# Nine landing buffers for gathered expert rows, and the lower parts of expert tiles shared between GpSimd and VectorE

## The chip, the core and the metric

The kernel runs on one core of one Trainium2 chip. The metric is the device time of one execution in microseconds (us), from the first instruction to the last; lower is better. The engines are TensorE (PE, with its weight loads as PEld), VectorE (DVE), ScalarE (ACT), GpSimd (POOL) and SyncE (SP). SP, ACT and POOL also issue DMAs.

## The reference, cut to what matters

One layer for 512 prompt tokens and 32 sample tokens (width 1024): two kinds of attention, then PEER, a layer of 128 x 128 = 16384 experts that are one neuron each. Only PEER matters here:

```python
def peer(x):                       # 544 tokens
    q = x @ w_query                # 8 heads; two halves scored against 128 sub keys each
    v1, i1 = top_k(s1, 16); v2, i2 = top_k(s2, 16)
    cand = v1[..., :, None] + v2[..., None, :]
    top, pos = top_k(cand, 16)     # 16 experts per head: 128 per token
    eidx = i1 * 128 + i2           # taken at pos
    g = softmax(top)
    hid = einsum("thkd,td->thk", u_tab[eidx], x)
    a = g * gelu(hid)
    return einsum("thk,thkd->td", a, v_tab[eidx])
```

## The kernel before, in words

**Two ways through the experts.** The last 384 prompt tokens take the dense way: TensorE multiplies them with all 128 tiles of the up table (a tile is 128 experts x 1024), ScalarE applies gelu, and the result goes to DRAM (`hidden_values`). A gate matrix, made from one-hots of the expert numbers, goes to DRAM too (`gate_matrix`), and a later stage multiplies both and the value table `v`. The first 128 prompt tokens and the 32 sample tokens take the sparse way: their expert rows are gathered one by one. A "row" of that work is 5 gathers (`ROW`): 4 for prompt tokens, 1 for the sample tokens spread over 128 partitions; each gather brings 128 table rows of 4 KB into one buffer of `gb`. There are 32 such rows (`SR`), 160 gathers, and for each a **dot** on VectorE (`dot`, L1837 to L1843): buffer times the tokens' activations in PSUM (`x2p`), summed.

**float32 products in three passes.** TensorE multiplies rounded parts. A tile `uw` is split into `uhi` (ScalarE rounds it, `u_split_hi`, L1317) and `ulo = uw - uhi` (`u_split_lo` on GpSimd, L1322, or `split_lo` on VectorE, L1851), and `mm3` (L224 to L228) adds hi*hi, lo*hi and hi*lo. `uhi` and `ulo` have two buffers each, `uw` has four (`UR`). So tile m+2 can be rounded only when product m is done, and its `ulo` has to be there when product m+1 is.

**The query stage** (the block from L1410) runs eight turns with 4 tiles each, then a tail of 16 tiles (`QX`). GpSimd makes every `ulo` here. VectorE picks the experts. In the tail ScalarE turns the gate logits into exponentials after tile 11 (`MIX = 11`, L1518 to L1520), which needs another activation table than gelu; VectorE normalizes them; SP spreads the sample tokens' indices and gates over the partitions; VectorE writes the first five rows of indices (`idx_row`, L1670), and GpSimd issues the first five gathers between its last splits. A block ends when all engines have ended.

**The gate stage** (the block from L1737) has 72 tiles in six turns of 12 (`GTI`), two turns to a pass of a hardware loop for the first four and the last two written out, and then 8 more tiles (`GX`), here called the tail. Per turn of 12 tiles:

- TensorE does the 12 products in halves and, between them, 16 groups of four one-hot products (L1778).
- VectorE does for each tile: the split `ulo` of tile i+2; the one-hots of one or two groups (`build_one_hots`: `oh` L1830, `og` L1831; every second group has its `oh` from ScalarE); two dots (three in the last tile), 25 in a turn.
- ScalarE does gelu and its store (L1340, L1342), `uhi` (L1320), the eviction of each group (L1936), half of the `oh` (L1910, L1914), and twice a turn the store of 2 MB of gates (L1927).
- GpSimd issues a gather as soon as the dot that frees its buffer is done (`fetch_u_row`, L1363): five gathers are under way or waiting for VectorE. It cuts the one-hots' numbers twice a turn (`cut`, L1791).
- SP loads the tiles `uw`. At the stage's start it also loads four value tiles into `vw`.

The tail's 8 products come with no groups. VectorE does the last ten dots there, three to a tile, then the lower parts of the four value tiles, then the last split. Its last lines wait for the first products with the gates. ScalarE ends the block with a wait for all gelu stores (L1963, L1964). The value stage (from L1998) then takes its first tiles at once.

## Time and profile before

| | us |
|---|---|
| three runs | 1894.58, 1899.97, 1898.62 (median 1898.62) |
| the profiled execution, its own time | 1890.6 |
| its span, first to last instruction | 1889.0 |
| TensorE busy in the span | 1715.0 (91%) |
| VectorE busy | 1400.6 (74%) |
| ScalarE busy | 783.8 (41%) |
| GpSimd busy | 594.3 (31%) |

The mean TensorE clock granted is 0.956 of full speed. The parts of the span that are spoken of below: the end of the query stage, from about 805 to 838 us; the gate stage's 72 tiles from 838.4 to 1287.1 us; its tail to 1328.3 us; a wait between blocks to 1338.6 us; then the value stage to the end, 550 us.

A group of instructions is named by line, engine, operation, the tile that it writes and the tiles that it reads. In a timeline, the first column is the start in us, the second what it took, and in brackets stands how long the engine had been idle before it and what ended that.

### The profile page before, as it was taken

To read this page: it belongs to the slowest core of one execution; us is meant where nothing else is said; L and a number is where in the kernel's file an instruction comes from. 1 tells how busy PE (TensorE), PEld (TensorE's weight loads), DVE (VectorE), ACT (ScalarE), POOL (GpSimd) and SP (SyncE) were. 2 spreads that over 40 slices of the span, in tenths; PEclk is the share of its full clock that TensorE was granted. 3 is DMA by queue.
4 is the path that set the end of the run, shared out by engine and by line. 5 is a ranking of instruction groups with operands and counts; after the bars stand their busy time and mean duration, and the time that the engine had idled before them with its cause. 6 is when DMAs were issued, how large, how long until landed. Compare 5 with 4: busy or idle time off the path is not lost. (4 is left out here: it accounts for less than half of the span.)

```text
span 1889.0 us, 30318 instructions
## 1 busy us (share of the span) xinstructions
PE 1715.0 (91%) x9914; PEld 1501.5 (79%) x9914; DVE 1400.6 (74%) x3171; ACT 783.8 (41%) x1195; POOL 594.3 (31%) x516
## 2 busy tenths in 40 slices
PE   5997898789799999979889899998799999999995
PEld 4997643449699999969889898997688888888883
DVE  3334267534399999939898898997799999999994
ACT  3231044211434342337566576664233333333333
POOL 0010270000344534633333334333333333333330
PEclk9998899889799999989999999998899999999997
DMA  3352461260343432458999999999999999999991
GB/s 110 98 181 80 138 192 46 107 242 5 119 148 103 147 99 96 158 204 320 345 330 338 342 360 343 373 367 332 341 382 384 384 384 384 384 386 386 387 383 62
DMA packets 195215, 470.82 MB, mean 249 GB/s; under 512 B 17922, under 2 KB 100482, under 8 KB 192558
## 3 DMA queue, kind: packets, MB, share of 16 engines
q1 hardware_dynamic: 124014, 240.30, 36.5%
q0 software_dynamic: 50944, 178.96, 25.6%
q10 hardware_dynamic: 20160, 50.34, 6.7%
q8 instruction: 52, 0.85, 0.2%
q14 instruction: 45, 0.37, 0.1%
HBM read 411.97 MB, written 61.32 MB: 251 GB/s over the span
## 5 line engine op out<-in xcount | busy, mean ns | idle before, releaser
L226 PE MATMUL hp<-mid_hi,uhi 128*128 128x384 f32 x1024 | 361.4, 353 | 23.6 <-DVE ulo L1853 8.5
L227 PE MATMUL hp<-mid_lo,uhi 128*128 128x384 f32 x1024 | 351.1, 343 | 0.0
L228 PE MATMUL hp<-mid_hi,ulo 128*128 128x384 f32 x1024 | 349.7, 342 | 0.0
L226 PE MATMUL va<-vhi,ahi 128*128 128x512 f32 x768 | 299.8, 390 | 10.4 <-PEq L1734 10.4
L228 PE MATMUL va<-vhi,alo 128*128 128x512 f32 x768 | 299.5, 390 | 0.0
L227 PE MATMUL va<-vlo,ahi 128*128 128x512 f32 x768 | 299.5, 390 | 0.0
L1712 POOL DMA_INDIRECT gathered<-in_v_experts,idx_row x160 | 189.2, 1183 | 329.2 <-DVEq L2060 284.9
L1369 POOL DMA_INDIRECT gathered<-in_u_rows,idx_row x160 | 171.8, 1074 | 299.5 <-DVE hrow L1840 208.1
L1720 ACT ACTIVATE vhi<-vw 128x1024 fp32r<-128x1024 f32 x128 | 135.9, 1062 | 256.8 <-PE va L228 145.3
L226 PEld LDWEIGHTS hp<-mid_hi,uhi 128*128 128x128 f32 x1024 | 198.4, 194 | 28.7 <-issue 15.5
L1320 ACT ACTIVATE uhi<-uw 128x1024 fp32r<-128x1024 f32 x128 | 135.6, 1059 | 167.1 <-PE hp L228 114.6
L227 PEld LDWEIGHTS hp<-mid_lo,uhi 128*128 128x128 f32 x1024 | 198.3, 194 | 0.0
L228 PEld LDWEIGHTS hp<-mid_hi,ulo 128*128 128x128 f32 x1024 | 197.7, 193 | 0.0
L1840 DVE CUSTOM_DVE_ANT_0 gathered<-gathered,x2p 128x1024 f32<-128x1024 f32 x150 | 177.9, 1215 | 22.9 <-DMA gathered<-in_u_rows,idx_row 20.2
L226 PEld LDWEIGHTS va<-vhi,ahi 128*128 128x128 f32 x768 | 144.7, 188 | 40.7 <-issue 10.7
L1324 POOL TENSOR_TENSOR ulo<-uw,uhi 128x1024 fp32r<-128x1024 f32 x50 | 125.0, 2501 | 148.8 <-ACT uhi L1320 148.8
L227 PEld LDWEIGHTS va<-vlo,ahi 128*128 128x128 f32 x768 | 144.7, 188 | 30.1
L228 PEld LDWEIGHTS va<-vhi,alo 128*128 128x128 f32 x768 | 144.6, 188 | 30.1
L1724 DVE TENSOR_TENSOR vlo<-vw,vhi 128x1024 fp32r<-128x1024 f32 x128 | 156.1, 1221 | 12.9 <-ACT vhi L1720 11.8
L2057 DVE SCALAR_TENSOR_TENSOR acc<-gathered,crow,acc 128x1024 f32<-128x1024 f32 x128 | 164.1, 1282 | 0.7 <-DVE acc L2057 0.7
L1778 PE MATMUL ggp<-og,oh 128*128 128x128 f32 x768 | 106.8, 283 | 30.4 <-DVE og L1831 29.6
L1778 PEld LDWEIGHTS ggp<-og,oh 128*128 128x128 f32 x768 | 97.8, 193 | 43.0 <-DVE og L1831 25.7
(331 smaller groups left out, 3281.8 us busy)
## 6 DMA issues: line engine op xcount, KB each, us to landing
uw<-in_u_experts SPq DMA_DIRECT2D x128, 512.0 KB
vw<-in_v_experts SPq DMA_DIRECT2D x128, 512.0 KB
hidden_values<-gelu_out ACTq DMA_DIRECT2D x128, 192.0 KB
gate_matrix<-gst ACTq DMA_DIRECT2D x12, 2048.0 KB
hd<-hidden_values SPq DMA_DIRECT2D x16, 768.0 KB
gt<-gate_matrix SPq DMA_DIRECT2D x16, 768.0 KB
uw<-hidden_values SPq DMA_DIRECT2D x16, 768.0 KB
uw<-gate_matrix SPq DMA_DIRECT2D x16, 768.0 KB
```

The lines of the kernel that those rows point to most:

```text
L226: nc.tensor.matmul(out, a_hi, b_hi, start=first, stop=False)
L227: nc.tensor.matmul(out, a_hi, b_lo, start=False, stop=False)
L228: return nc.tensor.matmul(out, a_lo, b_hi, start=False, stop=last)
L1320: nc.scalar.activation(uhi[:, i], uw[:, r], ACT.Copy).then_inc(u_hi, 1)
L1324: nc.gpsimd.tensor_tensor(ulo[:, i], uw[:, r], uhi[:, i].bitcast(F32), ALU.subtract).then_inc(u_lo, 1)
L1369: nc.gpsimd.indirect_dma_start(gb[:, b], None, u_table, bass.IndirectOffsetOnAxis(ap=idx_row[:, slot, b:b + 1], axis=0)).then_inc(gathered ...
L1712: nc.gpsimd.indirect_dma_start(gb[:, b], None, v_table, bass.IndirectOffsetOnAxis(ap=idx_row[:, slot, b:b + 1], axis=0)).then_inc(gathered ...
L1720: nc.scalar.activation(vhi[:, c], vw[:, c], ACT.Copy).then_inc(xs["vhi"], 1)
L1724: nc.vector.tensor_tensor(vlo[:, c], vw[:, c], vhi[:, c].bitcast(F32), ALU.subtract).then_inc(xs["vlo"], 1)
L1778: last = nc.tensor.matmul(gp[i % 2][:, k], oh[:, i % RING, k], og[:, i % RING, k], start=True, stop=True)
L1840: nc.vector.tensor_tensor_reduce(out=gb[:, b], in0=gb[:, b], in1=x2p[:, b // SG], scale=1.0, scalar=0.0, op0=ALU.mult, op1=ALU.add, accum_ ...
L2057: nc.vector.scalar_tensor_tensor(acc0[:], gb[:, c], crow[:, q, c:c + 1], acc0[:], ALU.mult, ALU.add).then_inc(s["s0"], 1)
```

## The change

Five things change together.

1. **Nine buffers.** The four `vw` buffers, idle in the gate stage, join the five of `gb` (`buffers`, `LOOK = 9`). Nine rows of indices are prepared, nine gathers are issued at the end of the query stage, and a gather waits for the dot nine before it. Five dots now stand ahead of the turns (`FIRST_DOTS`), a turn has 25 and 20 dots in alternation (25 in each of the last two), and 15 instead of 10 stand in the tail. These 15 gathers use only the five `gb` buffers. The four value tiles are loaded when dot 145 is done, not at the stage's start.
2. **The splits.** In the 72 tiles GpSimd makes `ulo` at every odd i, VectorE at every even i. At the query stage's end VectorE makes two that were GpSimd's, and the last one moves behind the barrier, to the head of the gate stage.
3. **The exponential** comes after tile 13 (`MIX = QX - 3`), and two more `uw` loads stand before the spreading of the indices on SP.
4. **The wait for all gelu stores** goes from ScalarE at the end of the block to SP at the start of the value stage.
5. The value stage's gathers have semaphores of their own (no effect on the work).

The core of the diff:

```diff
-        MIX = 11
+        MIX = QX - 3
+        buffers = [gb[:, b] for b in range(ROW)] + [vw[:, i] for i in range(GT)]
+        FIRST_DOTS = ROW
+        TURN_ROWS = (ROW, ROW - 1)
...
-                for e in range(QX):
+                for e in range(QX - 3):
                     u_split_lo(pool, RT * NH + e + 2, e % 2, (e + 2) % UR)
-                    if e == QX - 3:
-                        for b in range(3):
-                            fetch_u_row(pool, 0, 0, b)
-                    if e == QX - 2:
-                        for b in range(3, ROW):
-                            fetch_u_row(pool, 0, 0, b)
+                for n in range(LOOK):
+                    request(pool, n)
...
 # GpSimd, a turn of the gate stage
-                        while at < RJ * ROW * (i + 1) // GTI:
-                            q, b = divmod(at, ROW)
-                            fetch_u_row(pool, RJ * j + q + 1, (q + 1) % RJ, b)
+                        if i % 2:
+                            m = G0 + GTI * j + i + 2
+                            pool.wait_ge(u_lo, m + 2)
+                            u_split_lo(pool, m, i % 2, slot(half, i + 2))
+                        while at < n * (i + 1) // GTI:
+                            ahead = half * ROW * ROW + at + LOOK
+                            if not last or ahead < 2 * ROW * ROW:
+                                request(pool, FIRST_DOTS + ahead, pair)
...
 # VectorE, a turn of the gate stage
-                        split_lo(G0 + GTI * j + i + 2, i % 2, slot(half, i + 2))
+                        if i % 2 == 0:
+                            dve.wait_ge(u_lo, G0 + GTI * j + i + 4)
+                            split_lo(G0 + GTI * j + i + 2, i % 2, slot(half, i + 2))
...
 # VectorE, head of the gate stage
+                dve.wait_ge(s["x2p"], 2)
+                split_lo(G0 + 1, 1, 1)
+                for n in range(FIRST_DOTS):
+                    dot(n, hid[:, n // ROW, n % ROW:n % ROW + 1])
                 for i in range(AHEAD):
                     build_one_hots(0, i)
...
 # ScalarE, end of the gate stage
-                for i in range(2):
-                    act.wait_ge(ge_stored[i], 8 * NK + 16)
...
 # SP, gate stage
-                for i in range(GT):
-                    sp.dma_start(vw[:, i], A["v_experts"][i]).then_inc(vld[i], 16)
...
+                    if e == UR + 1:
+                        sp.wait_ge(s["dot"], TAIL)
+                        for i in range(GT):
+                            sp.dma_start(vw[:, i], A["v_experts"][i]).then_inc(vld[i], 16)
```

**GpSimd's order in a turn.** The first tiles of a turn in the loop. Before, it has the cut and gathers alone (rows that only compute a wait's value are the `ISA` and `REGISTER_ALU` ones):

```order
L1796 COPY chunkT<-slotT 128x96
L1367 REGISTER_ALU
L1369 DMA gathered<-in_u_rows,idx_row 128x1024
L1367 REGISTER_ALU
L1369 DMA gathered<-in_u_rows,idx_row 128x1024
L1367 REGISTER_ALU
L1369 DMA gathered<-in_u_rows,idx_row 128x1024
```

and now:

```order
L1829 COPY chunkT<-slotT 128x96
L1842 ISA
L1324 REGISTER_ALU
L1325 TENSOR_TENSOR ulo<-uw,uhi 128x1024
L1377 REGISTER_ALU
L1383 DMA vw<-in_u_rows,idx_row 128x1024
L1377 REGISTER_ALU
L1383 DMA vw<-in_u_rows,idx_row 128x1024
L1377 REGISTER_ALU
L1383 DMA gathered<-in_u_rows,idx_row 128x1024
L1377 REGISTER_ALU
L1383 DMA gathered<-in_u_rows,idx_row 128x1024
```

A split now stands behind the gathers of the tile before it and ahead of those of its own tile: four gathers (of an odd and an even tile), then the next split.

**VectorE's order at the head of the gate stage.** Before, right behind the barrier:

```order
L1830 TENSOR_SCALAR oh<-iota,chunkT 128x128
L1831 TENSOR_SCALAR og<-iota,chunkT 128x128
L1830 TENSOR_SCALAR oh<-iota,chunkT 128x128
L1831 TENSOR_SCALAR og<-iota,chunkT 128x128
L1830 TENSOR_SCALAR oh<-iota,chunkT 128x128
```

and now:

```order
L1897 TENSOR_TENSOR ulo<-uw,uhi 128x1024
L1397 ISA gathered,hid<-gathered,x2p 128x1024
L1397 ISA hid 128x1
L1397 ISA gathered,hid<-gathered,x2p 128x1024
L1397 ISA hid 128x1
```

The first one-hots move behind one split and five dots (an `ISA` row that reads `gathered` and `x2p`, and the short one that reads its sum, are one dot).

## Rows read from the trace of the kernel before

**Rows 1.** Stretches: us, busy (count) of PE, PEld, DVE, ACT, POOL; PEclk; DMA share; GB/s.

```profile
838.40:1287.10 448.70, 413.37 (x2522) 399.82 (x2523) 396.31 (x979) 292.43 (x480) 162.51 (x158) 0.97 0.93 344
1287.10:1338.60 51.50, 32.65 (x168) 31.08 (x167) 29.47 (x46) 16.20 (x24) 15.93 (x14) 0.84 0.94 358
...
1600.00:1700.00 100.00, 100.00 (x442) 82.78 (x442) 92.06 (x111) 37.35 (x49) 35.41 (x31) 1.00 1.05 384
```

**Rows 2.** Waits in 840:1290: who waited for whom, us, times, longest.

```profile
DVE gathered L1840 <- DMA gathered<-in_u_rows,idx_row: 20.2, 12, 3.7
ACT gelu_out L1340 <- DMA hidden_values<-gelu_out: 17.3, 5, 4.4
```

**Rows 3.** Timeline, one event in the gate stage, and TensorE at the loop's jump back.

```profile
927.09 1.22 DVE L1840 CUSTOM_DVE_ANT_0 gathered<-gathered,x2p 128x1024 f32<-128x1024 f32 x1 [3.53 <-DMA gathered<-in_u_rows,idx_row]
928.54 0.49 ACT L1340 ACTIVATE gelu_out<-hp 128x384 f32<-128x384 f32 x1 [3.48 <-DMA hidden_values<-gelu_out]
930.77 2.05 PE L1778 MATMUL ggp<-og,oh 128*128 128x128 f32 x8 [4.77 <-DVE og L1831]
991.42 0.68 PE L226 MATMUL hp<-mid_hi,uhi 128*128 128x384 f32 x1 [4.94 <-issue]
```

**Rows 4.** ScalarE's timeline: gelu after three tiles in a row, one `uhi`, the next gelu.

```profile
1102.17 0.49 ACT L1340 ACTIVATE gelu_out<-hp 128x384 f32<-128x384 f32 x1 [0.95 <-PE hp L228]
1107.80 0.49 ACT L1340 ACTIVATE gelu_out<-hp 128x384 f32<-128x384 f32 x1 [0.78 <-PE hp L228]
1108.96 1.06 ACT L1320 ACTIVATE uhi<-uw 128x1024 fp32r<-128x1024 f32 x1 [0.66 <-ACT gelu_out L1340]
1119.19 0.49 ACT L1340 ACTIVATE gelu_out<-hp 128x384 f32<-128x384 f32 x1 [1.02 <-PE hp L228]
```

**Rows 5.** Timeline, VectorE from one split to the next, and GpSimd's two gathers.

```profile
1104.70 1.22 DVE L1853 TENSOR_TENSOR ulo<-uw,uhi 128x1024 fp32r<-128x1024 f32 x1
1110.95 1.22 DVE L1853 TENSOR_TENSOR ulo<-uw,uhi 128x1024 fp32r<-128x1024 f32 x1
1104.37 0.94 POOL L1369 DMA_INDIRECT gathered<-in_u_rows,idx_row  x1 [2.44 <-DVE hrow L1840]
1105.62 1.11 POOL L1369 DMA_INDIRECT gathered<-in_u_rows,idx_row  x1 [0.30 <-issue]
```

**Rows 6.** One line each: instances, ns min/median/max, first and last start.

```profile
L1324 POOL TENSOR_TENSOR ulo<-uw,uhi x50: 2347/2406/3516, 494.1 to 832.6; 128x1024 fp32r<-128x1024 f32 x50
L1641 DVE TENSOR_TENSOR pk<-eq x8: 324/326/2303, 549.1 to 805.3; 128x160 f32<-128x160 bf16 x8
```

**Rows 7.** Timeline, GpSimd and VectorE: splits, and VectorE's two operations of the same size.

```profile
808.61 0.83 DVE L1651 TENSOR_TENSOR GG<-GG,first 128x640 f32<-128x640 f32 x1
811.23 2.36 POOL L1324 TENSOR_TENSOR ulo<-uw,uhi 128x1024 fp32r<-128x1024 f32 x1 [3.83 <-ACT uhi L1320]
811.53 2.75 DVE L1663 TENSOR_TENSOR GG<-GG,sm 128x640 f32<-128x640 f32 x1
```

**Rows 8.** Timeline, end of the query stage: ScalarE, GpSimd, TensorE.

```profile
809.47 0.74 ACT L1520 ACTIVATE GG<-GG 128x640 f32<-128x640 f32 x1 [2.59 <-DVE GG L1651]
832.63 2.35 POOL L1324 TENSOR_TENSOR ulo<-uw,uhi 128x1024 fp32r<-128x1024 f32 x1
838.42 0.68 PE L226 MATMUL hp<-mid_hi,uhi 128*128 128x384 f32 x1 [8.34 <-PEq L1372]
```

**Rows 9.** Timeline, the tail: VectorE, TensorE, ScalarE's last gelu and next work.

```profile
1289.98 1.22 DVE L1853 TENSOR_TENSOR ulo<-uw,uhi 128x1024 fp32r<-128x1024 f32 x1
1295.87 1.22 DVE L1880 CUSTOM_DVE_ANT_0 gathered<-gathered,x2p 128x1024 f32<-128x1024 f32 x1 [4.66 <-DMA gathered<-in_u_rows,idx_row]
1303.34 0.69 PE L226 MATMUL hp<-mid_hi,uhi 128*128 128x384 f32 x1 [7.65 <-DVE ulo L1853]
1328.29 0.49 ACT L1340 ACTIVATE gelu_out<-hp 128x384 f32<-128x384 f32 x1 [1.68 <-PE hp L228]
1338.47 1.03 ACT L2027 ACTIVATE acc<-h 128x1024 f32<-128x1024 f32 x1 [9.69 <-PEq L1734]
```

More of the change, by code:

```diff
@@ L1696, in build @@
         vld = [sem(f"x_vld{i}") for i in range(GT)]
+        row_landed = [sem(f"x_row{b}") for b in range(ROW)]
         gld = [sem(f"x_gld{i}") for i in range(2)]
@@ L1770, in _, with turn @@
                 pe.sem_inc(s["mm"], RING)
-                def turn(j, half, last):
+                def turn(pair, half, last):
+                    j = 2 * pair + half
                     def group(i):
@@ L1796, in cut, with turn @@
                     nc.gpsimd.tensor_copy(chunkT[:, u], slotT[:, :, bass.ds((2 * j + u) * CH, CH)]).then_inc(s["cut"], 1)
-                def turn(j, half, last):
+                def turn(pair, half, last):
+                    j = 2 * pair + half
+                    n = (ROW if last else TURN_ROWS[half]) * ROW
                     at = 0
@@ L1916, in _, with turn @@
                 first_one_hot(0, 1)
-                def turn(j, half, last):
+                def turn(pair, half, last):
+                    j = 2 * pair + half
                     def tile(i, part):
@@ L1939, in group @@
                             first_one_hot(j, i + 2)
-                        elif i % 2 and not last:
+                        elif i % 2 and not (last and half):
                             first_one_hot(j + 1, i + 2 - N2)
@@ L1962, in _, with turn @@
                             round_a(act, c, c, 0)
[L1963 to L1964 removed]
             @block.sync
             def _(sp):
[L1968 to L1970 removed]
+                def turn(pair, half, last):
+                    j = 2 * pair + half
                     for i in range(GTI):
```

134 lines of the change are left out of this document (83 added, 51 removed).

## The prediction, made before the run

> **What bounds the kernel now.** I first cut the span into stretches. The gate stage's 72 tiles take 448.7 us, with TensorE busy for 413 and VectorE for 396, the DMA engines at a share of 0.93; the 51.5 us behind them hold only 32.7 us of TensorE [rows 1]. So neither engine alone fills the stage. Next I took the pitch of undisturbed tiles from ScalarE's timeline, where each gelu starts when its product is done: three tiles, from 1102.17 to 1119.19, take 17.02 us [rows 4]. 24 such groups would be 408.5 us, so about 40 us are lost. Of these I see three kinds in the timelines. The first product runs at TensorE's lower clock (3 us), and at the loop's jump back TensorE stands for 4.94 us with nothing to wait for and starts at half speed (0.68 us for a matmul), together about 6 [rows 3]; neither is touched. Of the other 31 us, small gaps take some 3, and 28 stand around ten places where VectorE waits for a gather. In all it waits 20.2 us in 12 places, and ScalarE 17.3 us in 5 places for its own gelu stores [rows 2]. The largest shows how this counts: VectorE waits 3.53 us, the one-hots come late, TensorE stands for 4.77 us and starts again at half speed (2.05 us for a group that takes 1.13 otherwise, the 1.2 GHz level) [rows 3].
>
> **The change, part by part.** The sum is made against the profiled execution, 1890.6 us (span 1889.0). That is 8.0 us under the median of the three runs; I add these at the end.
>
> *End of the query stage: -1 us.* ScalarE no longer waits 2.59 us for the logits after tile 11 [rows 8], and two `uw` loads come earlier. But the block ends with its last engine. Before, that was GpSimd with a split (832.63 + 2.35); 3.4 us later TensorE starts, at 838.42 [rows 8]. Now GpSimd has nine gathers to issue, 1.25 us each [rows 5], 11.5 us in all, and it can start only when the indices are there. The exponential (now near 815), sum, reciprocal, product, the new split of 1.2 us and the spreading of the gates bring these to about 822. 822 + 11.5 = 833.5, against 835.0. The ends are -4 and +3.
>
> *Head of the gate stage: +3 us.* VectorE waits for `uhi` (1.1), then does one split and five dots (1.14 each) and only then the first one-hots. The first group is ready about 10 us after the start. TensorE's first product, at the low clock, is done after 7.3 us. Ends: +1 and +6.
>
> *Nine buffers: -20 us.* A buffer is asked for again nine dots ahead, not five; a dot comes every 2.7 to 3 us, so a gather has some 25 us, not 14, to land, and the waits of up to 3.7 us [rows 2] go. What is late next is ScalarE's own wait: two gelu buffers, and a gelu store that queues behind 2 MB of gates. In rows 3 it stands beside the gather's wait (3.48 us). It delays `uhi` and the evictions, and I leave 8 us of the 28 for it: five places, 1.6 each. The traffic does not fall: 25 gathers of 0.52 MB, twelve tiles and the stores are 26 MB a turn, at the value stage's 384 GB/s [rows 1] 67 us, just a turn of 68. Ends: -30 (all goes, and with it the cold clock), -10 (ScalarE's waits grow, as the gather queue is never empty).
>
> *Lighter VectorE: -3 us.* In clean groups TensorE still waits 0.26 us for `og`, once in three tiles; with six splits fewer a turn this and a little more goes. Ends -6 and 0.
>
> *Splits on GpSimd: +17 us.* This is the term I weigh most. The split itself takes 2.41 us there [rows 6] instead of 1.2. I laid out six tiles. A product's end is P; gelu starts at P + 0.1, `uhi` starts 1.16 later (1107.80 to 1108.96) and is done at P + 2.3 [rows 4], 0.7 later where ScalarE evicts. The split must be done when the next product ends, P + 6.0 to 6.4. Alone, GpSimd would be in time: 2.3 + 2.5 = 4.8. But the gathers of the even tile before stand ahead of it, and they wait for VectorE's dots. VectorE begins an even tile with its split at P + 2.2 and, where the tile has two groups, ends its dots 6.25 later (1104.70 to 1110.95 [rows 5]), at P + 8.45. GpSimd has the second gather issued some 2.1 after the last dot (the dot ends just before the split at 1104.70, the gather at 1105.62 + 1.11 = 1106.73 [rows 5]), at P + 10.55. Its split ends at P + 13.1. The next product's end, 5.4 later, plus 6.0 gives a due time of P + 11.4. TensorE waits 1.7 us. In the two other pairs of the six tiles the same sum comes out at or just under the due time. So 1.7 us per six tiles, 12 times: 20 us. Some of it falls together with ScalarE's waits; I take 17. Ends: 3 (requests in time, as VectorE runs ahead) and 38 (the lock below in each pair).
>
> The port: VectorE's `pk` takes 326 ns, and 2303 once [rows 6]; in that one a GpSimd split was under way. Of two equal operations on `GG`, one took 0.83 us and the other, begun 0.3 us after a GpSimd split, 2.75: it ended 0.7 after the split had [rows 7]. So a VectorE operation with two inputs in SBUF stands still behind a GpSimd split. In the gate stage the dots have one input in PSUM, and the two engines' splits exclude each other in time anyway. For the one-hots the trace shows no such pair; the sum assumes a loss inside the slack that VectorE gains. The Trainium skill (SBUF - State Buffer, "Who interferes with whom") says more: a `tensor_scalar` in a 2-port mode contends with GpSimd as well, and whoever comes first blocks the other fully. By that rule every GpSimd split that meets one-hots holds VectorE up to 2.4 us; this is the second rival below.
>
> *The tail: +3 us.* Before, from the last of the 72 products to the value stage's start it took 51.5 us [rows 1]: 41.2 to the last product, then ScalarE's wait for all gelu stores, which held the block from 1328.8 to about 1335 (its next work is at 1338.47 [rows 9]). That wait now delays no engine but SP: -7. Against this, the queue of gathers runs dry: the first of the last 15 waits for dot 145, some 6 us behind product 72. 15 gathers are 7.9 MB; four value tiles, now in the same stretch, are 2.1; `uw` loads, first gates and gelu stores some 4. 14 MB at 0.384 MB/us [rows 1] is 36 us, so the last gather lands near 42 us. Then come a dot, four lower parts of value tiles (4.6), the last split, a product (4.2), the barrier (3.4): 57 us, so +6. The other end is -7, if gathers come as asked. I take +3, nearer to the ledger; upper end +10. The waits before the last products (4.66 us, with TensorE idle for 7.65 [rows 9]) turn into more and shorter ones.
>
> *The value stage* has the same work. SP's wait for gelu stores ends before the tiles of the third group are due: 0.
>
> Sum: -1 + 3 - 20 - 3 + 17 + 3 = -1. 1890.6 - 1 + 8.0 = **1897.6 us**, no change that can be measured. A measurement of this kernel can tell about 0.3% (5.7 us) from nothing.
>
> **The rivals.** *Waits gone, GpSimd in time.* If VectorE's dots run ahead (B turns have only 20), or the gathers are issued faster, the 17 shrinks to about 3 and the 20 grows to 26: with the tail at 0 this is -27 us, 1871. For it: 36 splits of 1.2 us leave VectorE's 396 us [rows 1]; gathers are the largest wait. Against it: VectorE's even tile always begins with a split that waits for `uhi`, so it can't run ahead there.
>
> *GpSimd's queue and the lock (slower).* The place is the odd tile, the price is what the split waits for. If one-hots are held too, VectorE loses 2.4 us in two of three pairs: 4.8 - 3.5 (the splits given away) = 1.3 us more work per six tiles than before, each late one-hot stops TensorE, and the clock falls behind long waits. With 38 for 17 and the gathers' gain at 15, the sum is +26: 1924. It decides as soon as the wait before every second `ulo` is over 2.5 us per six tiles. For it: rows 6 and 7. Against it: by my layout most GpSimd splits lie beside dots.
>
> *The gathers were not the cause.* If the losses come from ScalarE's store waits, nine buffers bring only -5; with a share of the rest this is +12, 1910. For it: five of the large losses have both waits. Against it: five small ones have only the gather's.
>
> **How the numbers follow.** The balance as summed: 0.37 (inside it a third each falls to faster, same, slower, the same a little more). Waits gone: 0.32. Queue and lock: 0.19. Store waits: 0.12, all slower. Faster by over 0.3%: 0.32 + 0.11 = 0.43. Within: 0.17, with 0.02 from the rivals' edges 0.19. Slower: 0.38. The range reaches from the faster rival with the tail's other end (-7 us: 1864) to the slower rival (1924); beyond either I leave one in ten.
>
> **What would show it.** Right: VectorE's waits for gathers in the 72 tiles fall from 20 us to under 4; GpSimd's `ulo` starts 1 to 3 us after its `uhi` in the odd tile behind two groups, and TensorE's idle time names GpSimd's `ulo` with 10 to 25 us; the first one-hots come 8 us after the barrier; from product 72 to the value stage 50 to 58 us. Wrong: three tiles in 16.8 us throughout, no wait on GpSimd's `ulo` (faster); or one-hots of over 1 us beside GpSimd splits and a stage over 460 us (slower).

## The result: slower, and where the time went

The changed kernel takes 1912.97 us, the median of five runs (1910.02 to 1915.19), against 1898.62 for the kernel before in the same series. The ratio is 1.0084, with a 95% interval from 1.0071 to 1.0098: 14.4 us, or 0.84%, slower. That lies inside the recorded range, but it is neither the forecast (no change) nor the side to which most of the chance was given.

The profiled run of the changed kernel is 1912.35 us (span 1910.8). The profiled run of before was 8.0 us under its median, so the two spans differ by 21.8 us where the medians differ by 14.4. The ledger below explains the 21.8, and up to 7 us of it are scatter.

The stretches of the changed kernel, which answer to [rows 1]: from TensorE's first product of the gate stage to the gelu that the prediction took as the end of 72 tiles (by count of gelus it is the one behind product 73, in both kernels), and from there to the value stage. The columns are start and end, length, busy time and count of PE, PEld, DVE, ACT and POOL, granted clock, DMA share, GB/s.

```profile
843.00:1296.95 453.95, 409.78 (x2522) 398.51 (x2523) 417.91 (x935) 294.30 (x482) 225.34 (x183) 0.98 0.91 326
1296.95:1360.00 63.05, 33.38 (x168) 31.78 (x166) 34.73 (x54) 16.42 (x24) 23.40 (x21) 0.82 0.96 354
```

I go on calling them the 72 tiles and the tail. The 72 tiles grew by 5.3 us and the tail by 11.5. VectorE lost 36 splits of 1.2 us and is still busy for 21.6 us more.

The waits in the same part of the program (840 to 1300 us): who waited for whom, us in all, times, longest.

```profile
PE hp L226 <- POOL ulo L1325: 24.5, 19, 4.8
PE ggp L1811 <- DVE og L1873: 19.6, 15, 3.9
...
ACT gelu_out L1341 <- DMA hidden_values<-gelu_out: 4.5, 2, 3.0
```

VectorE's wait for gathers, 20.2 us in [rows 2], is gone from this list. In its place TensorE waits 24.5 us for lower parts that GpSimd makes.

The timeline of one such wait, in the changed kernel: start, length, engine, line, operation.

```profile
911.93 0.94 POOL L1383 DMA_INDIRECT gathered<-in_u_rows,idx_row  x1 [0.30 <-issue]
...
912.37 2.99 DVE L1872 TENSOR_SCALAR oh<-iota,chunkT 128x128 f32<-128x128 f32 x1
...
912.89 2.38 POOL L1325 TENSOR_TENSOR ulo<-uw,uhi 128x1024 fp32r<-128x1024 f32 x1
...
915.29 0.34 DVE L1873 TENSOR_SCALAR og<-iota,chunkT 128x128 f32<-128x128 f32 x1
915.33 0.44 PE L226 MATMUL hp<-mid_hi,uhi 128*128 128x384 f32 x1 [1.24 <-POOL ulo L1325]
```

Two things stand here together. GpSimd's split comes right behind a gather, and TensorE waits for it. And a one-hot of VectorE, 0.28 us elsewhere, lasts 2.99 us, until the split is done.

The end of the query stage and the tail, in the changed kernel's timeline, which answer to [rows 8, 9].

```profile
817.67 0.82 DVE L1690 TENSOR_REDUCE sm<-GG 128x40 f32<-128x640 f32 x1 [3.94 <-ACT GG L1545]
825.16 1.12 POOL L1383 DMA_INDIRECT gathered<-in_u_rows,idx_row  x1 [11.78 <-DVE idx_row L1702]
835.39 0.94 POOL L1383 DMA_INDIRECT vw<-in_u_rows,idx_row  x1 [0.30 <-issue]
842.66 0.26 POOL L1829 COPY chunkT<-slotT 128x96 f32<-128x96 f32 x1 [6.33 <-DVEq L1861]
843.00 0.68 PE L226 MATMUL hp<-mid_hi,uhi 128*128 128x384 f32 x1 [15.41 <-PEq L1400]
...
1298.31 0.95 POOL L1383 DMA_INDIRECT gathered<-in_u_rows,idx_row  x1 [2.11 <-DVE hrow L1397]
1308.57 1.22 DVE L1397 CUSTOM_DVE_ANT_0 gathered<-gathered,x2p 128x1024 f32<-128x1024 f32 x1 [8.21 <-DMA gathered<-in_u_rows,idx_row]
1316.60 0.69 PE L226 MATMUL hp<-mid_hi,uhi 128*128 128x384 f32 x1 [11.37 <-DVE ulo L1897]
```

The nine gathers start at 825.16, not at the 822 of the prediction, and end at 836.3. TensorE, whose last product was done at 827.3, stands for 15.4 us. The first one-hots follow a split and five dots, as forecast, and TensorE waits for them:

```profile
852.80 1.90 PE L1811 MATMUL ggp<-og,oh 128*128 128x128 f32 x8 [3.91 <-DVE og L1873]
```

In the tail the first of the last fifteen gathers is asked for at 1298.31, VectorE waits 8.21 us for its row, and TensorE 11.37 us for a split behind it. VectorE's last dot begins at 1337.34 and the last product ends at 1350.8. Then TensorE stands still once more, before its first product of the value stage:

```profile
1360.04 0.76 PE L226 MATMUL va<-vhi,ahi 128*128 128x512 f32 x1 [9.24 <-PEq L1767]
```

### The profile page after: what moved, and what is told of

It reads as the page before. It is cut to its first block and busy times, and to the rows that moved or that the text cites. A ratio compares the mean times of both kernels' runs of the same rounds, so it can differ in the third digit from the quotient of the medians.

```text
span 1910.8 us, 30365 instructions
## 1 busy us (share of the span) xinstructions
PE 1711.9 (90%) x9914; PEld 1500.2 (79%) x9914; DVE 1430.8 (75%) x3137; ACT 785.4 (41%) x1195; POOL 661.3 (35%) x549
## 5 line engine op out<-in xcount | busy, mean ns | idle before, releaser
L1325 POOL TENSOR_TENSOR ulo<-uw,uhi 128x1024 fp32r<-128x1024 f32 x83 | 204.5, 2464 | 155.7 <-ACT uhi L1321 155.0
L1383 POOL DMA_INDIRECT gathered<-in_u_rows,idx_row x96 | 98.1, 1022 | 150.2 <-DVE hrow L1397 93.9
L1990 ACT ACTIVATE gst<-ggp 128x512 f32<-128x512 f32 x96 | 108.5, 1130 | 61.9 <-PE ggp L1811 48.5
L1397 DVE CUSTOM_DVE_ANT_0 gathered<-gathered,x2p 128x1024 f32<-128x1024 f32 x96 | 114.6, 1216 | 17.1 <-DMA gathered<-in_u_rows,idx_row 15.4
L1873 DVE TENSOR_SCALAR og<-iota,chunkT 128x128 f32<-128x128 f32 x384 | 123.2, 365 | 0.0
```

Of the source, the lines that this page charges most:

```text
L1325: nc.gpsimd.tensor_tensor(ulo[:, i], uw[:, r], uhi[:, i].bitcast(F32), ALU.subtract).then_inc(u_lo, 1)
L1397: nc.vector.tensor_tensor_reduce(out=buffers[to], in0=buffers[to], in1=x2p[:, b // SG], scale=1.0, scalar=0.0, op0=ALU.mult, op1=ALU.add, ...
L1873: last = nc.vector.tensor_scalar(og[:, i % RING, k], iota[:], col(0), col(2), ALU.is_equal, ALU.mult)
L1990: nc.scalar.activation(gst[:, u, :, 4 * r:4 * r + 4].rearrange("p i t -> p t i"), gp[i % 2][:], ACT.Copy).then_inc(s["ev"], 1)
```

## The experiments

Each kernel was timed beside the kernel before in at least five rounds. Ratios are to the kernel before, with their 95% intervals; a gain from one experiment to the next is the difference of their ratios. The theories at the start: GpSimd's splits cost time, either because VectorE's operations stand still beside them, as at an SBUF port that both engines use (**P**, port), or by their place in GpSimd's queue (**Q**; experiments 1 and 2 do not part the two yet); and **B**, the gather waits were slack and the buffers bring nothing. Tail, head and barrier have theories of their own.

**1. All splits of the turns back on VectorE.** The changed kernel with this edit:

```diff
 # GpSimd's turn
-                        if i % 2:
...
-                            u_split_lo(pool, m, i % 2, slot(half, i + 2))
 # VectorE's turn
-                        if i % 2 == 0:
-                            dve.wait_ge(u_lo, G0 + GTI * j + i + 4)
-                            split_lo(G0 + GTI * j + i + 2, i % 2, slot(half, i + 2))
+                        split_lo(G0 + GTI * j + i + 2, i % 2, slot(half, i + 2))
```

> The changed kernel with one part undone: VectorE makes the lower parts of all 72 tiles in the turns again, and GpSimd none; nine buffers, the later exponential and the tail stay as changed. Theory P (port): GpSimd's splits cost the stage what the nine buffers give, since VectorE's one-hots stand still beside them (0.28 us became 3.00 us) and since a split stands behind gathers. VectorE then gets 36 splits of some 1.14 us back (41 us) and loses some 57 us of slowed one-hots; the 72 tiles take 435 to 445 us (453.9 in the changed kernel, 448.7 before), and the run 1898 to 1906 us. The rival B (buffers): the gather waits were slack of VectorE and the nine buffers bring nothing; the 72 tiles take 448 to 454 us and the run 1908 to 1914 us. In both the way from the last product of the turns to the value stage stays some 60 us.

Measured: 1.0041 (1.0028 to 1.0054), 1899.5 us. Its stretches, and the one kind of wait for a DMA in its 72 tiles:

```profile
843.99:1284.64 440.65, 414.35 (x2522) 400.40 (x2523) 391.05 (x969) 292.60 (x481) 146.57 (x147) 0.97 0.91 336
1284.64:1347.10 62.46, 35.15 (x169) 33.86 (x167) 35.52 (x56) 16.34 (x24) 23.11 (x21) 0.80 0.96 359
```

```profile
ACT gelu_out L1341 <- DMA hidden_values<-gelu_out: 19.2, 6, 4.7
```

The 72 tiles take 440.7 us: 13.3 under the changed kernel and 8.0 under the kernel before. Theory B falls. GpSimd's splits cost 13 us of this stretch, and 8 us by the ratios; the rest of the loss is in the tail (62.5 us) and at the end of the query stage.

**2. The splits on GpSimd alone,** on the kernel before, five buffers kept; the same lines as in experiment 1, put in.

> The kernel before with one part of the change alone: GpSimd makes the lower parts of every second tile in the turns, five buffers and all else as before. Theory P: slower than before by 10 to 25 us (1908 to 1924), some one-hots of VectorE last 1 to 3 us beside a split of GpSimd, and VectorE's busy time in the 72 tiles does not fall although it makes 36 splits fewer. Rival B: the splits on GpSimd are neutral, and the run stays at 1897 to 1901 us; the loss of the whole change then lies in its head and tail.

Measured: 1.0060 (1.0040 to 1.0081). The 72 tiles take 460.7 us, 12 more, although this profiled run was one of the kernel's fastest (1898.9). VectorE is busy for 425.7 us of them (396.3 before) with 36 splits fewer; TensorE waits 32.9 us for GpSimd's lower parts. So the splits cost about the same with five buffers (11 to 12 us) as with nine.

**3. The wait for the last gelu stores alone,** on the kernel before.

```diff
 # ScalarE, end of the gate block
-                for i in range(2):
-                    act.wait_ge(ge_stored[i], 8 * NK + 16)
 # SyncE, start of the value block
+                for i in range(2):
+                    sp.wait_ge(ge_stored[i], 8 * NK + 16)
```

> The kernel before with one part of the change alone: the wait for the two last gelu stores moves from the end of ScalarE's gate block to SyncE's start of the value block. By the prediction's term it gives 7 us back (1891 to 1893 us). The rival, by the changed kernel's trace, in which 9.2 us still lie between the last product and the first of the next block: the blocks' change itself takes that long, and the run stays at 1897 to 1900 us.

Measured: 0.9996 (0.9981 to 1.0011). Nothing comes back: TensorE still stands for 10.83 us ahead of the first value product (10.39 in the kernel before). A gain of 7 us would be a ratio of 0.9963 and lies outside the interval.

```profile
1341.15 0.77 PE L226 MATMUL va<-vhi,ahi 128*128 128x512 f32 x1 [10.83 <-PEq L1734]
```

**4. The order of the last buffers,** on the kernel of experiment 1.

```diff
-            users = [n for n in range(TAIL) if n % LOOK == t % ROW] + [TAIL + q for q in range(t % ROW, t, ROW)]
+            to = (t + 1) % ROW
+            users = [n for n in range(TAIL) if n % LOOK == to] + [TAIL + q for q in range(t % ROW, t, ROW)]
```

The gather goes to buffer `to`, and VectorE's dots of the tail take the same one (not shown).

> The first of these kernels (all splits of the turns on VectorE) with the last fifteen gathers sent to the buffers in the order 1, 2, 3, 4, 0 and not 0 to 4: the first of them then waits for dot 137 and not for dot 145, the fifth for 145. Theory T (dry queue): the tail is long because the first of the last gathers is behind the last dot of the turns; here four of them are under way by then, VectorE's wait of 8.2 us for the first row falls to under 2 us, the way from the last product of the turns to the value stage falls from some 60 to 50 to 55 us, and the run is 5 to 10 us below the first kernel. The rival: rows land no faster than one in 1.25 to 2.6 us beside the loads of the value experts, the first wait goes and later ones grow, and the run is within 2 us of the first kernel.

Measured: 0.9997 (0.9985 to 1.0009), 1891.6 us, 0.0044 or some 8 us below experiment 1. The profile shows both theories at work: the first wait is gone, and one of 4.52 us appears later. The stretch ends at 57.6 us, not at the 51.5 of [rows 1].

```profile
1281.05:1338.60 57.55, 34.98 (x168) 33.38 (x167) 35.52 (x56) 16.43 (x24) 19.34 (x17) 0.86 0.96 362
```

```profile
1294.65 1.22 DVE L1398 CUSTOM_DVE_ANT_0 gathered<-gathered,x2p 128x1024 f32<-128x1024 f32 x1 [4.52 <-DMA gathered<-in_u_rows,idx_row]
1296.69 0.94 POOL L1383 DMA_INDIRECT gathered<-in_u_rows,idx_row  x1 [4.81 <-DVE hid L1398]
...
1299.81 0.69 PE L226 MATMUL hp<-mid_hi,uhi 128*128 128x384 f32 x1 [6.29 <-DVE ulo L1894]
```

**5. The first one-hots ahead of the first five dots,** on experiment 4.

```diff
                 split_lo(G0 + 1, 1, 1)
+                for i in range(AHEAD):
+                    build_one_hots(0, i)
                 for n in range(FIRST_DOTS):
                     dot(n, hid[:, n // ROW, n % ROW:n % ROW + 1])
-                for i in range(AHEAD):
-                    build_one_hots(0, i)
```

> The same kernel (all splits on VectorE, new order of the last buffers, 1891.6 us) with VectorE's first two sets of one-hots ahead of its first five dots. In the one without, TensorE stood 3.9 us for the first set at 853.8 us and ran the group at half clock behind it (1.99 us and not 1.2). Theory H (head): that wait goes and the run is 3 to 5 us shorter (1887 to 1889). The rival: the wait only moves, since the five dots then stand ahead of the next split (5.7 us), and the run stays within 1 us.

Measured: 0.9962 (0.9946 to 0.9977); the 72 tiles fall from 439.5 to 433.3 us. The order at the head costs 6 us.

```profile
842.59:1275.89 433.30, 410.11 (x2522) 396.54 (x2523) 390.86 (x969) 292.14 (x481) 150.69 (x151) 0.98 0.94 346
```

**6. No gather ahead of the barrier,** on experiment 5: the loop over `request` moves from the query block to behind the first chunk copy of the gate block.

> The kernel with one-hots first, in which also all nine first gathers are asked for behind the barrier and the first chunk copy, not ahead of the barrier. Theory N (nine gathers): before the barrier GpSimd issues nine gathers in some 11.3 us from 825 us on, and the last product of the query stage ends at 828; without them TensorE starts the gate stage 7 to 10 us earlier (15.6 us of idle time become 6 to 8), the first rows land some 8 us later than now against the dots, and the run is 4 to 8 us shorter (1881 to 1885). The rival: the dots, 9 us later, hold up VectorE's splits in the first tiles, and the run is within 2 us of the kernel without.

Measured: 0.9929 (0.9910 to 0.9948), 0.0033 or 6 us below experiment 5. TensorE's idle time between the blocks falls from 15.9 to 1.9 us, and the stage starts 12.7 us earlier in the profile (829.86); but its 72 tiles take 442.8 us, not 433.3. Both theories are half right: the start is won, and 9.5 of the 12.7 us are given back in the profiles, about half by the ratios.

```profile
829.86:1272.65 442.79, 414.86 (x2522) 401.10 (x2523) 391.64 (x969) 292.05 (x481) 161.04 (x160) 0.97 0.94 349
```

**7. Gelu stores on SyncE's queue,** on experiment 6.

```diff
 # ScalarE's turn
-                            hidden_gelu(act, m, i % 2)
+                            hidden_gelu(act, m, i % 2, store=False)
 # SyncE's turn
+                        store_gelu(sp, G0 + GTI * j + i - 2, i % 2)
                         u_fetch(sp, G0 + GTI * j + i + UR, slot(half, i))
```

`store_gelu` waits for the gelu and stores its result; the first and last tiles, which are changed to match, are not shown.

The reason was the chain of one wait in experiment 1, in time order over four engines: a store of gates, the gelu that waits for an earlier gelu's store, VectorE behind it, TensorE behind that.

```profile
1140.47 0.34 ACTq L1975 DMA_DIRECT2D gate_matrix<-gst  x1
1155.65 0.49 ACT L1341 ACTIVATE gelu_out<-hp 128x384 f32<-128x384 f32 x1 [3.54 <-DMA hidden_values<-gelu_out]
1157.98 1.23 DVE L1893 TENSOR_TENSOR ulo<-uw,uhi 128x1024 fp32r<-128x1024 f32 x1 [2.70 <-ACT uhi L1321]
1161.08 2.07 PE L1811 MATMUL ggp<-og,oh 128*128 128x128 f32 x8 [2.68 <-DVE og L1869]
```

> The kernel with late requests, in which SyncE's queue stores the gelu results of the 72 tiles, not ScalarE's, on which they stand behind the 2 MB stores of the gate matrix. With all splits on VectorE there is one wait of ScalarE for a gelu store of 3.5 to 4.7 us per turn of twelve tiles, 15 us behind the issue of a gate store, and behind it TensorE stands 2.7 to 3.1 us for one-hots and runs eight matmuls at half clock (2.07 us and not 1.16). Theory S (stores): these waits go, and the run is 10 to 16 us shorter than without. The rival: the stores wait behind the 0.5 MB loads of expert tiles on SyncE's queue, or the DMA engines (0.92 busy) are what is short; the run is within 4 us.

Measured: 0.9779 (0.9757 to 0.9800), 1852.2 us: 28 us below experiment 6 and 42 below the kernel before. This is the version that beats both kernels.

```profile
833.82:1246.32 412.50, 399.98 (x2522) 394.12 (x2523) 390.30 (x969) 285.24 (x482) 156.39 (x160) 0.99 0.99 376
```

The 72 tiles take 412.5 us, 30.3 less than in experiment 6. TensorE's wait for `og`, 18.0 us there, is 2.9. The DMA share is 0.99; that the traffic is the next bound was not tried.

The gain is far above the 10 to 16 us expected, and the edit did more than its theory says. ScalarE's waits for gelu stores fall from 21.1 to 10.5 us only. But ScalarE had also stood some 0.6 us behind every gelu, to see it finished and to issue the store, before it could round the next tile. In experiment 6:

```profile
ACT uhi L1321 <- ACT gelu_out L1341: 41.1, 71, 0.7
```

In experiment 7 this wait is gone from the 72 tiles, and three tiles in a row with no disturbance take 16.35 us, where they took 17.06 (ScalarE's rows of the same tiles, experiment 6 and then 7):

```profile
941.53 0.49 ACT L1341 ACTIVATE gelu_out<-hp 128x384 f32<-128x384 f32 x1 [0.96 <-PE hp L228]
958.59 0.49 ACT L1341 ACTIVATE gelu_out<-hp 128x384 f32<-128x384 f32 x1 [1.03 <-PE hp L228]
...
939.90 0.49 ACT L1345 ACTIVATE gelu_out<-hp 128x384 f32<-128x384 f32 x1 [0.98 <-PE hp L228]
956.25 0.49 ACT L1345 ACTIVATE gelu_out<-hp 128x384 f32<-128x384 f32 x1 [1.05 <-PE hp L228]
```

Undisturbed threes are 0.5 to 0.7 us shorter throughout the stage, so by my estimate 12 to 17 of the 30 us come from the shorter cycle and the rest from the store waits. No run parts the two.

**8. Work on GpSimd that nobody waits for,** on experiment 4.

```diff
 # GpSimd's turn
+                        if i % 2:
+                            pool.wait_ge(spare_done, GTI // 2 * j + i // 2 + 1)
+                            nc.gpsimd.tensor_tensor(spare[:], spare[:], spare[:], ALU.subtract).then_inc(spare_done, 1)
```

> The kernel with all splits on VectorE and the new order of the last buffers (1891.6 us), in whose turns GpSimd also does, in every second tile where the changed kernel has its split, a subtraction of the same size over a buffer of its own that nobody waits for. It parts two ways in which GpSimd's splits cost: theory P (port): VectorE's one-hots stand still while GpSimd subtracts, whoever uses the result; then some one-hots last 1 to 3 us, VectorE's busy time in the 72 tiles rises by 40 us or more from 391 us, and the stage by 6 to 14 us (run 1897 to 1906). Theory Q (queue): the cost is TensorE's wait for a split that stands behind two gathers; nothing waits here, so the stage grows by 0 to 3 us (run 1890 to 1895), and one-hots beside GpSimd's work stay near 0.3 us.

Measured: 1.0306 (1.0282 to 1.0329), 59 us more than experiment 4, far beyond what either theory expected. VectorE and GpSimd in its timeline:

```profile
1014.21 2.72 DVE L1876 TENSOR_SCALAR og<-iota,chunkT 128x128 f32<-128x128 f32 x1
...
1014.94 1.90 POOL L1846 TENSOR_TENSOR spare<-spare 128x1024 f32<-128x1024 f32 x1
1016.85 0.27 DVE L1875 TENSOR_SCALAR oh<-iota,chunkT 128x128 f32<-128x128 f32 x1
```

```profile
850.22:1347.07 496.85, 423.95 (x2522) 407.77 (x2523) 464.91 (x969) 295.52 (x482) 217.30 (x189) 0.95 0.85 302
```

A one-hot lasts until GpSimd's subtraction is done. VectorE is busy for 74 us more than in experiment 4 (464.9 against 391.0) and the stage is 57 us longer (496.9 against 439.5). So the standstill needs no dependence at all between the two. The subtractions also stand in GpSimd's queue ahead of gathers, but that is not the cause here: in these 72 tiles VectorE never waits for a gather, while TensorE's wait for one-hots goes from 19.6 us in experiment 4 to this:

```profile
PE ggp L1813 <- DVE og L1876: 67.6, 46, 3.9
```

In this kernel VectorE has nothing given back for what it loses.

**9. Gelu stores on SyncE, on the kernel before,** five buffers.

> The kernel before, five buffers and all, with one edit that is no part of the change: SyncE's queue stores the gelu results of the 72 tiles. With nine buffers and all splits on VectorE this edit took the 72 tiles from 442.8 to 412.5 us. It tells what the ten waits for gathers of the kernel before were. Theory B (both causes): VectorE's gather waits come of five buffers, so they stay (some 20 us) and the run gains less than with nine, 8 to 18 us (1876 to 1886). Theory S (one cause): gathers landed late only because ScalarE's waits held VectorE and so the requests back, or because the 2 MB stores crowded the same queue; they go too, and the run gains 22 to 30 us (1864 to 1872), that is, nine buffers bring next to nothing beside it.

Measured: 0.9937 (0.9918 to 0.9956), theory "both causes". VectorE's gather waits stay:

```profile
DVE gathered L1845 <- DMA gathered<-in_u_rows,idx_row: 18.0, 10, 3.3
```

The 72 tiles take 434.6 us, 14 less than before, and 22 more than with nine buffers in experiment 7. Undisturbed threes are shorter here too (16.31 us for the tiles that took 17.03 before), and 24 times that 0.7 is more than the 14. So with five buffers the shorter cycle may be the whole gain.

**10. The same edit on the changed kernel.**

> The changed kernel whole, GpSimd's splits included, with the same single edit (SyncE's queue stores the gelu results of the 72 tiles). The changed kernel ran 1.0084 of before. Theory P (port): with the stores' waits gone VectorE is next, and GpSimd's splits take some 66 us of its time beside one-hots for the 41 us they give; the stage then keeps 10 us or more over the 412.5 of the kernel with all splits on VectorE, and the run gains 15 to 25 us on the changed kernel (ratio to before 0.995 to 1.001). The rival: once ScalarE does not wait, VectorE has slack for both, the stage takes 412 to 416 us and the run gains over 30 (ratio under 0.992).

Measured: 1.0046 (1.0031 to 1.0061), a gain of only 7 us, less than either side expected. The 72 tiles take 448.6 us with VectorE busy for 420.4: the stores' waits are gone (3.7 us left), and GpSimd's splits hold the stage.

**11 and 12. Two orders around experiment 7:** four first gathers ahead of the barrier, and fewer dots at the start of the tail.

> The kernel with stores on SyncE (ratio to before 0.978), in which four of the nine first gathers are again asked for ahead of the barrier and five behind it. Each takes GpSimd 1.25 us, and they can start at 825 us, as the last product of the query stage ends: so the gate stage starts some 5 us later than without them, and VectorE's first dots some 5 us earlier. Expected: within 3 us of the kernel without, if both count alike; 4 to 6 us slower if only the start of the stage counts, faster by 2 to 5 if the first dots' rows do.

> The kernel with stores on SyncE, in whose tail VectorE makes no dots behind its first split and 3, 4, 4 and 4 behind the next four, not 3 behind each of five. In the tail TensorE waits 6.6 us for a split that stands behind a dot whose row is late. If rows are what is late (dry queue), the wait moves from the fourth product to a later one and the run stays within 2 us; if the order is, TensorE's waits for splits in the tail fall from some 21 us to under 14 and the run by 4 to 7 us.

Measured: 0.9781 (0.9762 to 0.9800) and 0.9783 (0.9764 to 0.9801). Neither moved the time. In experiment 12 TensorE's waits for splits in the tail went from 15.4 to 14.4 us only. VectorE waited less for gathers (5.5 us, not 10.9) and as much more for `uhi` (6.2, not 0.7), so the order of these dots is not what holds the tail.

**13. The changed kernel with repairs 4, 5 and 6.**

> The changed kernel, GpSimd's splits included, with the three repairs that were measured one after the other on the kernel with all splits on VectorE: last buffers in the order 1, 2, 3, 4, 0 (ratio down by 0.0044), one-hots ahead of the first five dots (0.0035), all first gathers behind the barrier (0.0033). If the parts add up, 1.0084 becomes 0.996 to 0.999. If GpSimd's splits eat them (VectorE is the bound in the stage), the head's and the barrier's parts do not come through and it stays at 1.001 to 1.005.

Measured: 1.0047 (1.0029 to 1.0066). The parts do not add up: 7 us of the expected 21 come. The stage starts at 826.2, and its 72 tiles then take 460.0 us. The tail takes 62.5 us, hardly less than the 63.05 of the changed kernel, although its last buffers are in the new order. The first of the last fifteen gathers stands behind a split of GpSimd that waited 9.11 us for its `uhi`, and VectorE still waits for the row:

```profile
1283.06 2.42 POOL L1325 TENSOR_TENSOR ulo<-uw,uhi 128x1024 fp32r<-128x1024 f32 x1 [9.11 <-ACT uhi L1321]
...
1295.90 1.22 DVE L1398 CUSTOM_DVE_ANT_0 gathered<-gathered,x2p 128x1024 f32<-128x1024 f32 x1 [6.28 <-DMA gathered<-in_u_rows,idx_row]
```

**14. GpSimd's split ahead of the gathers,** on the changed kernel.

```diff
-                        if i % 2:
-                            m = G0 + GTI * j + i + 2
+                        if i % 2 == 0:
+                            m = G0 + GTI * j + i + 3
                             pool.wait_ge(u_lo, m + 2)
...
                         while at < n * (i + 1) // GTI:
```

> The changed kernel with GpSimd's split of every odd tile moved ahead of the two gathers of the tile before it, which wait for VectorE's dots. It parts the recorded term (the split stands behind gathers, 17 us) from the port. Theory Q (queue): TensorE's waits for GpSimd's lower parts in the 72 tiles (24.5 us in the changed kernel) fall under 8, the stage by 8 us or more, and the ratio to before from 1.0084 to 1.000 to 1.004. Theory P (port): the split then runs beside other work of VectorE or the same; the waits only change their name, one-hots of up to 3 us stay, and the ratio stays within 1.006 to 1.011.

Measured: 0.9994 (0.9976 to 1.0011), 17 us below the changed kernel: theory Q. Its stretch, and VectorE's one-hots in 840 to 1290 us (shapes, count, busy us, mean ns, idle before), first there, then in the changed kernel:

```profile
843.20:1280.45 437.25, 408.02 (x2522) 394.72 (x2523) 406.98 (x935) 293.66 (x481) 232.59 (x183) 0.98 0.91 339
```

```profile
L1873 DVE TENSOR_SCALAR og<-iota,chunkT 128x128 f32<-128x128 f32 x384 | 135.6, 396 | 0.0
L1872 DVE TENSOR_SCALAR oh<-iota,chunkT 128x128 f32<-128x128 f32 x192 | 78.2, 408 | 0.0
```

```profile
L1873 DVE TENSOR_SCALAR og<-iota,chunkT 128x128 f32<-128x128 f32 x380 | 122.1, 365 | 0.0
L1872 DVE TENSOR_SCALAR oh<-iota,chunkT 128x128 f32<-128x128 f32 x192 | 113.8, 593 | 0.0
```

TensorE no longer waits for GpSimd's lower parts at all, and the 72 tiles take 437.2 us and not 454.0. Yet the one-hots still stand still: in experiment 1 their means are 345 and 287 ns. So in the changed kernel the place in the queue costs most, and the standstill lies in the main inside the 41 us that VectorE was given. VectorE's busy time also fell, by 11 us; what of the 17 that made is not parted. This kernel is also 0.0047 below experiment 1, so 36 splits off VectorE are a gain of 3 us by the stretch and up to 9 by the ratios, if nothing waits for them.

**15 and 16. GpSimd's splits in the best kernel** (experiment 7), first in the changed kernel's order, then ahead of the gathers.

> The kernel with stores on SyncE and late requests (ratio to before 0.978) with one edit: GpSimd makes the lower parts of every second tile, as in the changed kernel. It is the price of these splits where nothing else stands in TensorE's way. By the port (66 us of VectorE's time for 41 us given back, and some 20 us of waits for the split itself), the 72 tiles take 435 to 450 us and not 412.5, and the ratio is 0.990 to 0.998. If VectorE has slack for it, under 0.984.

> The kernel with stores on SyncE, late requests and GpSimd's splits (ratio to before 0.9985), with each of these splits moved ahead of the two gathers of the tile before it, as in the run that took the changed kernel from 1.0084 to 0.9994. With all splits on VectorE this kernel ran 0.978, its VectorE busy for 390 of 412.5 us. Theory Q: the queue is the whole price, also here; the ratio falls to 0.976 to 0.981. Theory P: the one-hots' standstill (63 us of VectorE's time in the changed kernel with this order, against 41 us of splits given back) brings VectorE to some 410 us, at the stage's own length; the 72 tiles take 418 to 430 us and the ratio is 0.982 to 0.990.

Measured: 0.9985 (0.9970 to 1.0000) and 0.9890 (0.9868 to 0.9911), against 0.9779 without them. The two stretches:

```profile
824.77:1274.45 449.68, 406.35 (x2522) 396.29 (x2523) 416.12 (x935) 285.46 (x481) 239.85 (x193) 0.98 0.93 341
```

```profile
829.12:1259.57 430.45, 405.48 (x2522) 395.31 (x2523) 400.97 (x935) 286.68 (x481) 237.43 (x193) 0.98 0.95 356
```

With the stores moved the splits cost 37 us of stage, and 18 where they stand ahead of the gathers. About half is the queue, and the rest stays with either order, with VectorE busy for 11 us more than in experiment 7 (401.0 against 390.3) and its one-hots late here and there. That the rest is the standstill is not shown: no form of the one-hots that GpSimd does not hold up was run.

## Why the prediction was wrong

The steps of the sum, against the spans of the two profiled runs (+21.8 us):

| Step | Predicted | Measured | By |
|---|---|---|---|
| ahead of the query stage's end | 0 | +1.7 | an earlier `ulo` is this much later; scatter |
| end of the query stage | -1 | +2.9 | first product 838.42, now 843.00, less the 1.7 |
| head | +3 | +6.2 | experiment 5 |
| nine buffers | -20 | -14.2 | by subtraction: experiment 1 (-8.0), less the head's +6.2 |
| lighter VectorE | -3 | -3.4 | experiment 14 against 1 |
| splits behind gathers | +17 | +16.7 | experiment 14 |
| tail | +3 | +11.5 | 51.5, now 63.05 |
| value stage | 0 | +0.4 | 550.4, now 550.8 |

**The step that failed most is the tail, +3 and in fact +11.5.** The -7 in it, "That wait now delays no engine but SP: -7", is wrong: experiment 3 removes this wait alone and gains nothing. After the last product 7 to 11 us pass before the first value product in every kernel here, with the wait or without it, so what [rows 9] show as ScalarE's 9.69 us was the change of blocks and not the wait. What the change itself spends them on no run shows.

The queue that runs dry, against this, was priced well. The prediction let the last row land near 42 us into the tail and the last product end at 53.6; the last dot began at 40.4 and the last product ended at 53.9. But the sum of 57 us then took the change of blocks at 3.4 us, the figure of another change, and here it is 9.2: the same error as the -7. With it the sum is 63, and the tail took 63.05. The remaining 3 us are my choice of +3 against a ledger that said +6. Experiment 4 brings 8 us back by the order of the buffers with all splits on VectorE; in experiment 13, with GpSimd's splits, the same order brings under 1 us of tail.

**The end of the query stage: right place, wrong start and wrong end.** The gathers were to start at 822 and started at 825.16. The exponential came at 816.89 and not near 815 (the sum of the gates waited 3.94 us for it), the spreading of the gates over the partitions took 3.8 us, and the first gather began 1.0 us after its indices were written. And TensorE starts 6.7 us behind the last gather, not the 3.4 that stood behind a split; why is open. Experiment 6 shows what nine gathers in that place cost in the end: 6 us.

**The head: right mechanism, half the size.** The first group was ready at 852.80, 9.8 us after the start, as forecast. But TensorE then stood 3.91 us and ran the group at the 1.2 GHz level (1.90 us).

**Nine buffers: right sign, and the rest went where the prediction looked.** VectorE's gather waits are gone. ScalarE's waits for its gelu stores stay: 19.2 us in experiment 1, 17.3 before. Four of the six, of 3.5 to 4.7 us, end 15 to 16 us after the issue of a store of gates, and the one shown has some 3 us of TensorE's time and a group at half clock behind it. I left 8 us of the 28 for this; against the -14.2 it should have been some 14. The rival that put the loss on the stores (chance 0.12) had part of the cause: moved off ScalarE's queue they give 28 us with nine buffers, and 12 with five, but a part of both is the shorter cycle of experiment 7, which no rival named. The buffers, in turn, are worth some 20 us of stage once the stores are out of the way (434.6 against 412.5); this is an estimate, since the two kernels also differ in when the first gathers are asked for. The gather waits and the store waits covered for each other, as in [rows 3], where both end within 1.5 us.

**GpSimd's splits: right place and size.** The hand layout gave +17 and experiment 14 gives 16.7, though it also took 11 us off VectorE's busy time, so that the two agree so closely is partly luck. The observable holds too: TensorE's waits for GpSimd's `ulo` are 24.5 us in 19 places. The other half, that one-hots would mostly miss GpSimd's splits ("by my layout most GpSimd splits lie beside dots"), is wrong: `oh` went from 287 to 593 ns in the mean. By the row at 912.37, the 128x128 one-hot that takes 0.28 us alone took 2.99 us beside a split. The rule of the Trainium skill (SBUF - State Buffer, "Who interferes with whom") that was weighed there, that a `tensor_scalar` contends with GpSimd too and is blocked in full, agrees with this row and with experiment 8 as to the length of the standstill. Who came first these rows do not settle: by the profile's times VectorE's operation began 0.5 and 0.7 us before GpSimd's in them, and still lasted until its end. The standstill did not set the time here, because VectorE had been given 41 us of splits; the stage stayed at 454, under the 460 that was to mark this rival.

Against the medians the sum of -1 was off by 15.4 us: 8.5 from the tail, 5.8 from the buffers, 3.9 from the query stage's end, 3.2 from the head, and 1.4 from the other rows together; 7.4 go off again, and that is luck, since the profiled run of before lay 8.0 us under its median and that of the changed kernel only 0.6. The faster rival was also added up wrong: its terms (17 to 3, 20 to 26, the tail at 0) give -24 and 1875 us, not -27 and 1871.

## What to carry to other kernels

When two waits end within a microsecond of each other, removing one only shows the other: price a change by what remains with each of them gone, and look for the edit that takes both. An edit that moves a DMA's issue to another engine can also shorten the cycle of the engine that gave it up; compare undisturbed groups before the whole gain goes to the wait. Work moved to GpSimd has two prices, its place in GpSimd's queue behind whatever waits there, and the standstill of VectorE's operations beside it; measure the second with work that nobody waits for before counting VectorE's time as saved. An idle stretch between two blocks is not the last wait in the code until a run without that wait has shown it.

## What the runs showed of the hardware

- A VectorE `tensor_scalar` of 128x128 float32 (0.28 to 0.34 us alone) lasted until a GpSimd `tensor_tensor` that ran beside it was done: 2.99 us beside one of 2.38, and 2.72 beside one of 1.90 that had no dependence on it. Copies of 128x5 indices were slowed too: 163 ns in the mean in experiment 1, 779 in experiment 14. The dots, with one input in PSUM, stayed at 1.21 us in experiment 8.
- The change from the gate block to the value block holds TensorE for 7 to 11 us in all kernels here; with the last wait for stores removed it was 10.83 us, with it 10.39.
- Gelu stores that share ScalarE's queue with 2 MB stores of gates were waited for up to 4.7 us (experiment 1), some 15 us after the large store was issued; from SyncE's queue, in experiment 7, the waits were 2.5 us at most, and the DMA engines moved 376 GB/s in the stage, against 349 in experiment 6.
- Between a gelu and ScalarE's next operation, with the issue of the gelu's store between them, 0.6 us passed in the mean (41.1 us in 71 places, experiment 6).
- Indirect gathers in a row left GpSimd every 1.25 us (0.95 and 0.30 idle, from 827.87 on in the changed kernel).
